# Full chunk first behind two splits, ada chunks between convolutions, half-width fillers: four moves in a two-block transformer kernel

## The reference

```
# block two of first_block (i = 1)
hn = rms_norm(h, norm_pre[1])
q, k, v, f_logit, q_m, gate = split_cols(hn @ w_in_b, [768, 768, 768, 12, 256, 1024])
main = fox_mixer(q, k, v, f_logit, b_f)         # log forget gates, summed over the tokens
y = concatenate([main, mem_out]) * silu(gate)
h = h + rms_norm(y @ w_out[1], norm_post[1])    # the "out boundary": two norms one after the other
# second_block
mod = silu(c) @ ada_w[layer] + ada_b[layer]     # shifts, scales and gates of a layer
# odd_mixer
qk, v, og, gates = split(modulate(x) @ w_in, [1024, 2048, 3072])
qk = silu(causal_dwconv(qk, conv_w, conv_b))    # 4 taps
lf = log_sigmoid(gates[..., 8:] + gate_b)
```

## Time and profile before

| | |
|---|---|
| three runs, median | 2070.93 us (2070.88 to 2072.73) |
| the profiled execution, its own time | 2073.93 us |
| its span in the profile | 2072.2 us |
| mean granted TensorE clock | 0.99 |
| TensorE busy | 1991.6 us (96%), 10078 matmuls |
| VectorE, ScalarE, GpSimd busy | 1042.7, 776.8, 805.9 us |
| moved by DMA | 205.73 MB |

### The profile page before, as it was taken

How to read it: one execution, slowest core, us unless ns; L and a number is a source line. 1 busy time by engine, 2 the same in 40 slices (tenths; PEclk the granted TensorE clock), 3 DMA queues, 4 the chain that set the end, 5 groups by cost and what they waited for, 6 DMA issues and landing times.

```text
span 2072.2 us, 24182 instructions
## 1 busy us (share of the span) xinstructions
PE 1991.6 (96%) x10078; PEld 1559.7 (75%) x10078; DVE 1042.7 (50%) x1504; ACT 776.8 (37%) x1194; POOL 805.9 (39%) x342
## 2 busy tenths in 40 slices
PE   6999999899999999999999999998899999999998
PEld 5776667598766589977788888875887777788776
DVE  4523576654476657833566646667711342311323
ACT  3332664423465332156333213324257432322331
POOL 3433453243464263212334434343424334344342
PEclk8999999999999999999999999999999999999999
DMA  5323102155500343121333543452421113223221
GB/s 186 94 75 86 62 1 80 56 182 182 185 21 25 118 142 106 58 82 41 102 122 122 172 152 122 133 163 77 160 85 41 62 61 102 86 97 103 93 65 65
DMA packets 203405, 205.73 MB, mean 99 GB/s; under 512 B 12023, under 2 KB 199675, under 8 KB 203296
## 3 DMA queue, kind: packets, MB, share of 16 engines
q1 hardware_dynamic: 200953, 200.90, 30.4%
q0 software_dynamic: 1328, 3.13, 0.6%
q10 hardware_dynamic: 1015, 0.16, 0.0%
HBM read 201.20 MB, written 2.11 MB: 98 GB/s over the span
## 4 chain that ended last, share of the span: by engine, by line
PE 73%; DVE 10%; POOL 7%; ACT 7%; issue 2%; DMA 1%; SPq 0%; DVEq 0%; ACTq 0%
PE bank L530 41%; PE bank L1071 14%; POOL wl L2177 6%; ACT wh L1281 3%; PE bank L737 3%; PE bank L471 3%; PE bank L761 1%; DVE conv L2068 1%; DVE conv L2070 1%; PE bank L894 1%; PE bank L786 1%; DVE acc L1678 1%; DVE conv L2066 1%; PE bank L1128 1%; PE bank L1138 1%
## 5 line engine op out<-in xcount | busy, mean ns | idle before, releaser
L2177 POOL TENSOR_TENSOR wl<-ring,wh 128x2048 fp32r<-128x2048 f32 (+3 forms) x150 | 656.7, 4379 | 978.9 <-ACT wh L1281 978.9
L1281 ACT ACTIVATE wh<-ring 128x2048 fp32r<-128x2048 f32 (+3 forms) x150 | 265.2, 1769 | 238.3 <-PE bank L1071 130.0
L1678 DVE SCALAR_TENSOR_TENSOR acc<-ring,cs,acc 128x256 f32<-128x256 f32 x336 | 293.6, 874 | 12.0
L530 PE MATMUL bank<-xfh,wh 128*128 128x512 f32 x704 | 277.0, 394 | 11.0 <-POOL wl L2177 8.6
L530 PE MATMUL bank<-xfh,wl 128*128 128x512 f32 x704 | 274.2, 390 | 0.0
L530 PE MATMUL bank<-xfl,wh 128*128 128x512 f32 x704 | 274.1, 389 | 0.0
L530 PEld LDWEIGHTS bank<-xfh,wh 128*128 128x128 f32 x704 | 132.1, 188 | 46.1 <-POOL wl L2177 17.1
L530 PEld LDWEIGHTS bank<-xfh,wl 128*128 128x128 f32 x704 | 132.1, 188 | 28.0
L530 PEld LDWEIGHTS bank<-xfl,wh 128*128 128x128 f32 x704 | 132.2, 188 | 26.4
L1071 PE MATMUL bank<-hsph,wh 128*128 128x512 f32 x352 | 138.2, 393 | 2.8 <-POOL wl L2177 2.7
L1071 PE MATMUL bank<-hsph,wl 128*128 128x512 f32 x352 | 137.1, 390 | 0.0
(11 more groups left out here) (389 smaller groups left out, 4192.1 us busy)
## 6 DMA issues: line engine op xcount, KB each, us to landing
ring<-in_ada_w SPq DMA_DIRECT2D x48, 1024.0 KB, 5.3
ring<-in_ffn_w_in SPq DMA_DIRECT2D x44, 1024.0 KB, 5.1
ring<-in_w_in_b SPq DMA_DIRECT2D x14, 1024.0 KB, 5.4
ring<-in_even_w_in SPq DMA_DIRECT2D x14, 1024.0 KB, 5.1
ring<-in_ffn_w_out SPq DMA_DIRECT2D x16, 768.0 KB, 4.3
ring<-in_odd_w_in SPq DMA_DIRECT2D x12, 1024.0 KB, 5.6
ring<-in_ffn_w_out SPq DMA_DIRECT2D x16, 640.0 KB, 4.1
ring<-in_w_out SPq DMA_DIRECT2D x8, 1024.0 KB, 5.5
```

The source lines that it names most:

```text
L530: mm = eng.matmul(o, l_, r_, start=(first and i == 0), stop=(last and i == 2))
L1281: eng.activation(wh[:, m % SPLIT, 0:w], ring[:, n % RING, 0:w], ACT.Copy).then_inc(wh_ready, 1)
L1678: ins = eng.scalar_tensor_tensor(out=s, in0=w[:, k, :], scalar=cs[:, k:k + 1], in1=s, op0=ALU.mult, op1=ALU.add)
L2177: eng.tensor_tensor(wl[:, m % SPLIT, 0:w], ring[:, n % RING, 0:w], wh[:, m % SPLIT, 0:w].bitcast(F32), ALU.subtract).then_inc(wl_ready, 1)
```

## The change

1. **Order of chunks.** In block two the first gate chunk now stands ahead of the forget chunk, and in the odd mixer the first qk chunk ahead of the gate rows. All engines' code follows: ScalarE empties the two tiles of that chunk first, and the three fillers ahead of `odd.qk` are gone. The ada chunks keep their places in the ring.
2. **Odd ada chunks.** VectorE does one ahead of the convolutions, one behind the fifth and one behind the eighth, where all three stood behind the eighth.
3. **Fillers.** The seven fillers between the sums of squares in `out_first` are 256 columns wide, where they were 512 (both boundaries).
4. **Low parts.** Ahead of the even mixer the low part of the second `even.qa` chunk waits until all sixteen adds to x are done (`x_added`). In the odd mixer GpSimd does the low parts of the last two qk and first v chunk ahead of the wait for the maxima, and all of the v chunks ahead of the wait for the convolutions.

```diff
-    add(k8("in_b.f", w, 3 * MAIN, 3 * MAIN + P))
-    add(k8("in_b.v", w, 2 * MAIN, 3 * MAIN) + k8("in_b.qm", w, 2316, 2572) + k8("in_b.gate", w, 2572, 3596) + k8("in_b.q", w, 0, MAIN)
-        + k8("in_b.k", w, MAIN, 2 * MAIN), (0,) + 13 * (1,))
+    gates = k8("in_b.gate", w, 2572, 3596)
+    add(gates[:1] + k8("in_b.f", w, 3 * MAIN, 3 * MAIN + P))
+    add(k8("in_b.v", w, 2 * MAIN, 3 * MAIN) + k8("in_b.qm", w, 2316, 2572) + gates[1:] + k8("in_b.q", w, 0, MAIN)
+        + k8("in_b.k", w, MAIN, 2 * MAIN), 13 * (1,))
...
-    add(k8("odd.gates", w, 3008, 3088) + k8("odd.qk", w, 0, 1024) + k8("odd.v", w, 1024, 2048)
+    add(k8("odd.qk", w, 0, 256) + k8("odd.gates", w, 3008, 3088) + k8("odd.qk", w, 256, 1024) + k8("odd.v", w, 1024, 2048)
         + k8("odd.og", w, 2048, 3072), 5 * (0,) + 3 * (1,))
...
-                    eng.matmul(b[:, :], ident, consts[:, 0:S], start=True, stop=True)
+                    eng.matmul(b[:, 0:n], ident, consts[:, 0:n], start=True, stop=True)
...
                 for t in range(KT):
                     ssq(t, KT)
-                    warm(int(t < KT - 1))
+                    warm(int(t < KT - 1), n=S // 2)
...
+            project("in_b.gate", 1, "act", "x_b", xb)
             m, ws = chunk("in_b.f")
...
-            project("in_b.gate", 4, "act", "x_b", xb, lag=1)
+            project("in_b.gate", 3, "act", "x_b", xb, lag=1, t=2)
...
+            project("odd.qk", 1, "act", "x_odd", xo)
             m, ws = chunk("odd.gates")
...
-            project("odd.qk", 4, "act", "x_odd", xo, fill=3)
+            project("odd.qk", 3, "act", "x_odd", xo, t=2)
...
+            ada_steps(1)
             dve.wait_ge(qk_pads, 1)
             for t in range(KT):
...
-            ada_steps(3)
+                if t in (4, 7):
+                    ada_steps(1)
...
             attention(1)
+            low_weights(mark["att1"] + 5)
+            pool.wait_ge(x_added, 2 * KT)
             low_weights(mark["att1"] + 6)
...
-            low_weights(tile_chunk[index[("odd.qk", 5)]] + 2)
+            low_weights(tile_chunk[index[("odd.qk", KT - 1)]] + 2)
             pool.wait_ge(m_ready, 1)
             eng.dma_start(maxima, grow[5][0:ML_HEADS, :]).then_inc(maxima_stored, 16)
-            low_weights(tile_chunk[index[("odd.v", 0, NB - 1)]] + 2)
+            low_weights(tile_chunk[index[("odd.v", 2, NB - 1)]] + 2)
             pool.wait_ge(maxima_stored, 16)
             pool.wait_ge(qk_conv, KT)
```

More of the change, by code:

```diff
@@ L459, in opened_at, with warm @@
                 return opened(key, owner, place[1])
-            def warm(count, aside=False):
+            def warm(count, aside=False, n=S):
                 if not count:
@@ L599, in wide, with project @@
                             done(mm)
-            def project(stage, nchunks, owner, ready, xs, tok=False, lag=None, fill=0):
-                t = 0
+            def project(stage, nchunks, owner, ready, xs, tok=False, lag=None, fill=0, t=0):
                 warm(fill)
@@ L1444, in log_of @@
                 eng.activation(rows, rows, ACT.Ln, bias=1.0).then_inc(sem_out, 1)
+            for t in range(2):
+                empty(("in_b.gate", t), gate[:, t, :], ACT.Silu)
             act.wait_ge(loaded_p, 48)
@@ L1456, in _ @@
                 empty(("in_b.qm", t), qm[:, t, :])
-            for t in range(KT):
+            for t in range(2, KT):
                 empty(("in_b.gate", t), gate[:, t, :], ACT.Silu)
-                if t >= 2:
-                    act.wait_ge(frows_set, 32)
-                    act.wait_ge(frows_ready, 1)
-                    for h in (2 * t - 4, 2 * t - 3):
-                        eng.dma_start(qf[HD:HD + 1, h, :], frow[h:h + 1, 3, :]).then_inc(frows_moved, 16)
-                        eng.dma_start(kf[HD + 1:HD + 2, h, :], frow[h:h + 1, 4, :]).then_inc(frows_moved, 16)
+                act.wait_ge(frows_set, 32)
+                act.wait_ge(frows_ready, 1)
+                for h in (2 * t - 4, 2 * t - 3):
+                    eng.dma_start(qf[HD:HD + 1, h, :], frow[h:h + 1, 3, :]).then_inc(frows_moved, 16)
+                    eng.dma_start(kf[HD + 1:HD + 2, h, :], frow[h:h + 1, 4, :]).then_inc(frows_moved, 16)
             for name, dst, scale in (("in_b.q", qf, HD ** -0.5), ("in_b.k", kf, 1.0)):
@@ L1598, in _ @@
             shift(1, 0, tmp_o, xo)
+            for t in range(2):
+                empty(("odd.qk", t), qk_raw[:, t, 3:3 + S])
             empty(("og_rows",), grow[0][0:16, :], ACT.Identity, part=(slice(64, 80), slice(0, S)), bias=bf[0:16, 1:2])
```

## The result

The changed kernel takes 2057.29 us in the median of 4 runs (2055.39 to 2059.32), the kernel before 2071.27 (2070.88 to 2072.73, 4 runs); the ratio is 0.9929, with a 95% interval of 0.9916 to 0.9941. It is 14.0 us faster where 21.9 were forecast, and the median lies 1.3 us above the predicted range. The profiled execution took 2058.26 us.

The account below looks back on a forecast made before the run. TensorE's matmuls were taken as the bound, with time won only where it idles, runs fillers or runs at the lower clock. 5.4 + 1.5 + 0.3 + 14.7 = 21.9 us off the median 2070.93 gave 2049.0, range 2041 to 2056.

Parts of the forecast that it names:

- First boundary: Out boundary before the second mixer: half-width fillers and a shorter low part gain 5.4 us, between 4 and 6.
- Second boundary: Out boundary before the even mixer: first add freed, scaling row held by the delayed low part; gain 1.5 us, 0 to 6.5.
- Rival A: Second boundary: VectorE's scaling row gets the port before GpSimd's low part; 5 us more gained, 2044 us; chance 0.22.
- The wait of 7: Odd mixer: TensorE's 7.02 us wait for a low part, of the fourth value chunk, was claimed to go.
- rival D: Odd mixer: the 7.02 us wait and its low clock stay, the first ada chunk's load being late; 2059 us; chance 0.05.
- C: Rival: fillers no longer hold the clock, TensorE stays at 1.2 GHz from the boundaries into the product; 2082 us; chance 0.03.
- Rival B: Odd mixer: second ada chunk late, TensorE waits for the fourth value chunk, 5 us less; block two 2 less; 2056; chance 0.15.
- three microseconds of cover: Odd mixer: the fourth value chunk's low part is ready at 1494 and wanted at 1497.
- Block two: Full gate chunk ahead of the forget chunk: gains less two new waits, net 0.3 us, between -2 and +4.
- The first wait: Block two: with two split buffers, the first value chunk's low part comes late; 1.9 us lost.
- the second wait: Block two: the third value chunk's load waits for the ada chunk, so its low part is late; 3.3 us lost.
- Sum lost 4.8, gain 14.7 us: Odd mixer: 19.5 us of losses go, new low-part waits of 1.7 and 3.1 come; bounds 10 to 17.

Follow-up runs that it names:

- e1: The changed kernel run again without an edit, as the measure for the other runs: 2055.69 us, ratio 0.9917 to the kernel before.
- e6: The changed kernel with full-width fillers in the out boundaries again: 2060.04 us, ratio 0.9940 to the kernel before.
- e8: The changed kernel with the DMA that moves the gate rows issued by ScalarE right behind their emptying, not by GpSimd: 2050.67 us, ratio 0.9901.
- e9: The changed kernel with all three odd ada chunks behind the eight convolutions, as before the change: 2063.32 us, ratio 0.9963.
- e5: The changed kernel with the even boundary's delayed low part released by the scaling row instead of the last add to x: 2051.33 us, ratio 0.9901.
- e11: The changed kernel with the 1 MB ring load held back until the DMA of the gate rows has landed: 2055.25 us, ratio 0.9920.
- e7: The changed kernel without the delay of the low part ahead of the even mixer: 2056.08 us, ratio 0.9931.
- e4: The changed kernel with the third qk chunk's high part on ScalarE ahead of the gate rows' log chain: 2048.29 us, ratio 0.9882.

## Why the prediction was wrong

*Right.* **First boundary** (5.4): 5.1, by the path that was described, with the first add at 0.69, an idle time of 1.78, a pace of 1.20 and no fall of the clock. **Second boundary** (1.5): 1.3, with GpSimd first, the scaling row held for 4.63 and TensorE cold; 2.9 to 3.0 in e1, e6, e8 and e9, where the clock was up at the spread. Rival A is thereby out, though the margin was 0.04 us. **The wait of 7** went, as did the slow chunk behind it, so rival D is out. C is out too, since TensorE never stayed at the lower clock into a product; but the fillers don't always hold it: in the second boundary it fell among the narrow ones, behind a wait of 1.78, in e1, e5, e8 and e9. Rival B gave nearly the right time for a wrong reason: the three microseconds of cover held, and no value chunk waited.

*Right by luck.* **Block two** (0.3): 0.6 in the first profile, -2.0 in e1. The first wait is 1.78 for 1.9, and the step ahead of the ada chunk was held as foreseen (4.71). But the second wait is 1.25 where 3.3 was put, 2.0 less, 1.4 of it (against the 2.69 of e1) because the clock fell behind the first, which costs an estimated 1.7 that the sum doesn't have. The two errors cancel: 4.3 + 1.0 - 1.78 - 1.25 - 1.7 gives the 0.6. (The prediction's own terms give 4.3 + 1.0 - 1.9 - 3.3 = 0.1, not 0.3.)

*Wrong.* The step that failed is the odd mixer's "Sum lost 4.8, gain 14.7 us", in two of its terms.

1. "Low part ready by 1440 [...] while TensorE is free at 1437.0: 3.1 lost". The wait is 4.68. The 6.3 us from GpSimd's issue to the next high part were taken from the kernel before, where the DMA took 1.9 us; in the new place they are 8.6 (1420.63 to 1429.21), 2.2 of the difference in the move itself, which took 4.1. The low part that precedes it on GpSimd also releases a 1 MB ring load beside it, but with that load held back (e11) the move still took 3.6. So the term is wrong by the DMA's duration in its new place, of which the load is the smaller part; the cause of the larger part stays open.
2. No clock was charged to the new waits. Both were priced at their idle time alone, though the same text had charged 2.6 us for the clock behind the wait of 7.02 and up to 2.5 behind an idle time of 3.4. Behind the 4.68 it cost an estimated 3.1 us, and 1.5 to 2.9 behind the waits of 4.2 to 5.0 in e1, e5, e6, e7, e9 and e11 (mean clocks of 0.89 to 0.78 for 13.3 us). e4 takes away wait and clock together, e8 all but 1.83 of the wait: 6.8 and 4.7 us by the stretch.

With 1.72 + 4.68 + 3.1 = 9.5 lost in place of 4.8, the part's own sum gives 14.7 - 4.7 = 10.0; measured 9.4. That is 5.3 of the 6.2 us between the forecast 21.9 and the profiled 15.7. Of the rest, 0.9 is a stretch of lower clock in the feed-forward part (at 1343.6, behind a wait of 1.89 us), which the diff doesn't touch and which comes and goes from run to run in kernels that are the same there (680.2 or 681.6).

The last 1.7 us are in the comparison: the profiled execution of before was 2.7 above its median of four, that of after 1.0 above its own. 15.7 off one execution is 14.0 off the medians. The prediction took its gain off the median as if it carried over whole.

The range was too narrow at its upper end. Its bound of 10 for the odd part (cover gone, and a cold clock) was there in the text and is nearly what was measured (9.4), but the range's end came from rival B at 2056, which took 7 us off the gain and left out that a gain read from one execution can shrink against the medians.

## What to carry to other kernels

Price a new wait of TensorE as its idle time plus what the clock costs behind it, taken from a row behind a wait of similar length, and give it a range: here the clock stood at 1.00 behind the waits of up to 1.4 us, fell or held behind those of 1.4 to 2.6 by place and run, and was lower behind every one from 2.7 us up. Look too at what a fall hides: a clock lost early can shorten the next wait, and the sum then comes out right for the wrong reason. When a small DMA is moved behind another instruction, don't carry its duration over (1.9 us in the old place, 3.6 to 5.0 in the new one), and put nothing on the critical path behind it that could go ahead of it: one line that put a high part ahead of it was worth 7 us. When work is delayed to keep it out of another engine's way, release it by the last operation that it could hold, not by the one before.

## What the runs showed of the hardware

- The clock behind a wait depends on the run. One and the same kernel, behind a first wait of 1.78 or 1.80 us, ran on at a mean of 0.87 or 1.00 for 13.3 us; where it had been slower, its next wait was 1.25 and kept 1.00, where not, 2.69 and fell to 0.83. Both had the low part at the same moment. Place matters as well: behind 1.78 the clock fell in seven of eleven profiles in block two, in four of eleven in the second boundary and in none of twelve in the first. Second boundary: an idle time of 3.02 was followed by a spread of 2.08 us, and in the repeated run 2.57 by one of 1.16.
- A 16 KB move issued by GpSimd took 1.9 us alone, 4.1 beside a 1 MB load and an instruction fetch of 16 KB, and 3.6 with that load held back but the fetch at the same moment (3.8 to 5.0 in the other kernels that issue it behind the low part). The fetch's share was not separated. Issued by ScalarE ahead of both, it let ScalarE go on after 2.1.
- A two-input operation of 0.68 us on VectorE took 9.52 when GpSimd ran two low parts in a row: it was held across both. This is not a rule: e5 and e11 show the same 9.52, but in e1, e6, e7 and e9 VectorE got its turn between the two low parts (about 4.8), and the next two-input operation was held by the second. In e1:

```profile
1429.62 4.83 DVE L2108 TENSOR_TENSOR grow<-grow,grow 8x512 f32<-8x512 f32 x1
1434.48 5.56 DVE L2110 TENSOR_TENSOR_SCAN grow<-grow,grow 8x512 f32<-8x512 f32 x1
```

- A reciprocal (one input) beside a low part took its usual 0.95. The Trainium skill, SBUF — State Buffer, section "Who interferes with whom", counts only operations with two inputs or in a two-port mode among those that are held; the trace agrees (0.95 beside 4.63 for the two-input row). The one-input TENSOR_SCALAR ahead of block two's ada chunk was held too (4.71); whether it ran in a two-port mode no row shows.
